# A four-layer trunk with routed experts: the test for crowded groups moved behind the last scatter

## The reference, cut to what matters

```python
scores = jax.nn.sigmoid((t @ router_w).astype(jnp.float32))
sel = scores + router_b.astype(jnp.float32)
group_score = lax.top_k(sel.reshape(-1, N_GROUPS, EXPERTS_PER_GROUP), GROUP_SCORE_TOPK)[0].sum(-1)
best_group = jnp.argmax(group_score, axis=-1)          # one of 4 groups for each token
_, e_idx = lax.top_k(jnp.where(in_group, sel, -jnp.inf), TOP_K)   # two of its 4 experts
...
hid = jax.nn.silu(jnp.einsum("td,edf->tef", t, w_gate)) * jnp.einsum("td,edf->tef", t, w_up)
out = jnp.einsum("tef,efd->td", hid * combine[..., None], w_down)
...
xs = _layer_norm(ALPHA * xs + (1 + m_s[5])[:, None] * fs, ln_ffn_g[l], ln_ffn_b[l])
```

## Time and profile before

| | |
|---|---|
| median of three runs | 2169.0 us (2166.23 to 2172.78) |
| span of the profiled execution | 2165.3 us |
| TensorE busy (matmul / weight load) | 2015.4 / 1403.3 us |
| VectorE busy | 1336.2 us |
| ScalarE busy | 1028.3 us |
| GpSimd busy | 246.3 us |
| mean granted TensorE clock | 0.975 |
| chain that ended last | PE 75%, DVE 16%, ACT 4%, issue 3%, DMA 1% |

### The profile page before, as it was taken

How to read it: one execution, slowest core, us unless ns; L and a number is a source line. 1 busy time by engine, 2 the same in 40 slices (tenths; PEclk the granted TensorE clock), 3 DMA queues, 4 the chain that set the end, 5 groups by cost and what they waited for, 6 DMA issues and landing times.

```text
span 2165.3 us, 45010 instructions
## 1 busy us (share of the span) xinstructions
PE 2015.4 (93%) x18880; PEld 1403.3 (65%) x18881; DVE 1336.2 (62%) x2625; ACT 1028.3 (47%) x1779; POOL 246.3 (11%) x363
## 2 busy tenths in 40 slices
PE   6999999899998999899899998998999999989996
PEld 4666666557776676587656665776566666647774
DVE  3666666437896342689832325898666666538896
ACT  3344334226774251576523314766444444326774
POOL 1422222110001000100010001000322232100000
PEclk8999999999999999999999999999999999999998
DMA  9244334345896444488734353888311121125880
GB/s 396 88 164 147 123 139 166 143 139 207 281 326 220 146 158 190 156 306 299 261 124 154 119 214 136 303 302 308 104 64 62 49 70 46 46 81 192 281 305 31
DMA packets 56911, 381.21 MB, mean 176 GB/s; under 512 B 6400, under 2 KB 10624, under 8 KB 12144
## 3 DMA queue, kind: packets, MB, share of 16 engines
q1 hardware_dynamic: 51696, 373.00, 48.2%
q10 hardware_dynamic: 4608, 4.20, 0.6%
q0 software_dynamic: 384, 0.89, 0.1%
HBM read 373.96 MB, written 4.10 MB: 175 GB/s over the span
## 4 chain that ended last, share of the span: by engine, by line
PE 75%; DVE 16%; ACT 4%; issue 3%; DMA 1%; SPq 0%; DVEq 0%; ACTq 0%
PE ps L846 15%; DVE e_wlo L2843 7%; PE ps L1513 5%; PE ps L1517 4%; PE ps L1516 4%; PE ps L796 4%; PE ps L772 4%; PE ps L752 3%; PE ps L987 3%; DVE bufx L2862 3%; PE ps L1300 3%; PE ps L1469 2%; PE ps L807 2%; ACT e_whi L1708 2%; PE ps L1401 2%
## 5 line engine op out<-in xcount | busy, mean ns | idle before, releaser
L2843 DVE TENSOR_TENSOR e_wlo<-ring,e_whi 128x1024 fp32r<-128x1024 f32 x384 | 455.1, 1220 | 71.7 <-ACT e_whi L1708 70.2
L1708 ACT ACTIVATE e_whi<-ring 128x1024 fp32r<-128x1024 f32 x384 | 402.5, 1060 | 114.6 <-PE ps L1517 111.5
L846 PE MATMUL ps<-bufh,ring 128*128 128x384 f32 x1024 | 390.6, 503 | 2.2 <-ACT scratch L1708 0.7
L1513 PE MATMUL ps<-e_whi,e_hs 128*128 128x512 f32 x512 | 211.0, 412 | 35.5 <-DVE e_wlo L2843 32.4
L846 PEld LDWEIGHTS ps<-bufh,ring 128*128 128x128 f32 x1024 | 176.3, 190 | 93.5 <-issue 17.5
L1708 ACT ACTIVATE scratch<-ps 128x384 f32<-128x384 f32 (+6 forms) x311 | 109.1, 368 | 212.9 <-PE ps L846 53.0
L1517 PE MATMUL ps<-e_whi,e_hs 128*128 128x512 f32 x512 | 200.7, 392 | 0.0
L1516 PE MATMUL ps<-e_wlo,e_hs 128*128 128x512 f32 x512 | 200.0, 391 | 0.0
L2980 POOL TENSOR_SCALAR bufx<-bufo,x_gb 128x384 f32<-128x384 f32 x56 | 37.6, 686 | 1061.9 <-DVE bufo L2279 1061.9
L1513 PEld LDWEIGHTS ps<-e_whi,e_hs 128*128 128x128 f32 x512 | 96.0, 188 | 77.4 <-ACT e_whi L1708 51.9
L2372 DVE SCALAR_TENSOR_TENSOR scratch<-scratch,par 128x386 f32<-128x386 f32 x192 | 128.4, 669 | 4.8
(11 more groups left out here) (311 smaller groups left out, 3488.8 us busy)
## 6 DMA issues: line engine op xcount, KB each, us to landing
ring<-in_moe SPq DMA_DIRECT2D x192, 1024.0 KB, 4.9
ring<-in_w_ada SPq DMA_DIRECT2D x96, 1024.0 KB, 6.3
ring<-in_gdn_w_in SPq DMA_DIRECT2D x32, 1024.0 KB, 7.0
ring<-in_gdn_w_out SPq DMA_DIRECT2D x8, 1024.0 KB, 5.0
ring<-in_gqa_w_in SPq DMA_DIRECT2D x6, 1024.0 KB, 5.0
ring<-in_gqa_w_out SPq DMA_DIRECT2D x4, 1024.0 KB, 7.3
ring<-in_mla_w_out SPq DMA_DIRECT2D x4, 1024.0 KB, 8.1
ring<-in_mla_w_in SPq DMA_DIRECT2D x3, 1024.0 KB, 5.0
```

The costliest lines, as they stand in the source:

```text
L846: last = mm(ps[:, head_bank(n, m), 0:T], w[:, m % 2, kt, :], bufh[:, kt, :], start=(kt == 0), stop=(kt == KT - 1))
L1513: first = mm(out, parts[0], whi, start=start, stop=False)
L1708: return op(out, in_, ACT.Copy, **kw)
L2843: return tt_(e_wlo[:, b, :], w, e_whi[:, b, :].bitcast(F32), ALU.subtract)
```

## The change

On TensorE and VectorE the call of `crowded_blocks` moves from ahead of the last group's scatter to behind the whole list of steps, which ends with the last scatter (TensorE) and the last additions (VectorE). Inside the crowded part, TensorE now waits until the last group's additions are done too. ScalarE's program, the flags, the semaphore counts and all loads stay.

```diff
@@ -1563,7 +1563,7 @@
                 with pe.If(crowded > 0):
                     pe.wait_ge(F["yhi"], 2 * NG * (l + 1))
                     pe.wait_ge(F["ylo"], 2 * NG * (l + 1))
-                    pe.wait_ge(F["sc_ev"], KT * (NG * (l + 1) - 1))
+                    pe.wait_ge(F["sc_ev"], KT * NG * (l + 1))
                     with pe.Fori(0, NG) as g:
                         for b in range(2):
                             n = g * 2 + (2 * NG * l + b)
@@ -1676,11 +1676,10 @@
                     else:
                         n = NG * l + j
                         if e == 0:
-                            if j == NG - 1:
-                                crowded_blocks(l, comb)
                             pe.wait_ge(F["ga_ev"], 16 * l + 16)
                         scatter_piece(F, n, e, e_put[:, j % 2, :], (6, 0, 1, 2) if j == NG - 1 else (5, 6),
                                       n * KT if n else None)
+                crowded_blocks(l, comb)
 
             for S in (F, X):
                 pe.sem_inc(S["wfree"], SPLITS)
@@ -2931,13 +2930,12 @@
                     elif kind == "y":
                         y_low(F, NG * l + j)
                     elif kind == "s":
-                        if e == 0 and j == NG - 1:
-                            crowded_blocks(l)
                         if e == 0 and l + j:
                             dve.wait_ge(F["sc_ev"], KT * (NG * l + j))
                         scattered(F, l, NG * l + j, e, (6, 0, 1, 2) if j == NG - 1 else (5, 6))
                         if e == 3 and j < 2:
                             put_back(j + 2)
+                crowded_blocks(l)
 
             dve.wait_ge(params_in, 16)
```

## The result

The changed kernel takes 2177.93 us in the median of 17 runs, the kernel before 2168.83 in 17 runs; the ratio is 1.0035, with a 95% interval of 1.0023 to 1.0048, so 5 to 10 us more, some 7.6 (the two medians lie 9.1 apart). The forecast was 2177.3 and "slower".

The account below looks back on a forecast made before the run. It took the serial chain after each layer's last down products as the bound. Later column sums and fold cost 21.9 us, earlier additions win 13.6: +8.3, so 2177.3 as a median, range 2166 to 2185.

Parts of the forecast that it names:

- The gain: Last additions into bufx: start 1.49 us after the low part without the test ahead, winning 13.6 us over four layers.
- The place of the read: TensorE's flag read behind the last scatter tile: starts 2.85 us after the first addition.
- The length of the test: TensorE's flag read and branch before the column sums: 4.9 us in every layer, bounds 3.7 and 6.5.
- The sums: TensorE's eight column sums after the test: one piece at half clock, 3.3 us, from 2 x 1.74 less a tail.
- The fold: TensorE's fold after the column sums: about 1.55 us at half clock instead of 0.91, 0.64 more a layer.
- the kinder rival: TensorE's test and sums: clock or branch kinder than forecast, about 2170 us; chance 0.22.
- The sum: Whole kernel: 21.9 us lost less 13.6 won, +8.3 us.
- VectorE's test: Behind VectorE's last additions: free, covered by 3.1 us of TensorE's delay; without that cover up to 2.4 us a layer.
- second stop: Behind the branch's jump: none counted in the sum, though VectorE's row in layer 2 suggested one of about 2.9 us.
- The faster rival: TensorE's branch: jump target already in its buffer, branch under about 2.2 us, time about 2160 us; chance 0.08.

Follow-up runs that it names:

- the other execution of the kernel before: The kernel before, unchanged, executed once more for its trace; its four changed places took 50.53 us in all.
- the busy TensorE: Changed kernel plus four matrix products into an unread bank, queued on TensorE just ahead of the flag read; 2175.20 us, ratio to before 1.0022.
- eight banks: Changed kernel with eight PSUM banks instead of four for the last scatter; 2156.35 us, ratio to before 0.9948.
- the changed kernel's two executions: The changed kernel's profiled execution, spanning 2176.1 us, and one with 128 no-ops added at the head of TensorE's program, 2179.69 us in one run.
- the first experiment: Kernel before with only VectorE's test moved behind its last additions, TensorE's left ahead of the scatter; 2169.89 us, ratio to before 1.0004.

## Why the prediction was right, point by point

**The gain.** Right. The additions came 1.64 after the start of the low part in all four layers; forecast 1.49. The gain was 13.0 (5.40 + 5.79 + 4.77 + 3.58 - 4 x 1.64) instead of 13.6. TensorE's first weight load stands 0.91 after the start of the low part, not 0.74; the rest, 0.73, was as estimated.

**The place of the read.** Right: 2.76 after the first addition (676.0 - 673.24), forecast 2.85.

**The length of the test.** From the read to the first column sum 6.1, 4.6, 5.0 and 4.7 us, 5.1 in the mean, forecast 4.9. Right in the mean, but the reason holds only in part: I took layer 3's length for all because no weights would be loading. Hardly any were (8 and 0 GB/s by layer 0's stretches above), and layer 0's branch was 4.57 all the same. Where loads had run beside the branch before, it did get shorter by 0.4 to 0.5 (5.01 to 4.57, 3.75 to 3.37, 4.31 to 3.80), and in layer 3, which had none, it didn't (3.40 and 3.45). But in the other execution of the kernel before layer 3 took 3.92, so whether the loads or the place made the difference, no run separates.

**The sums.** Mis-sized: 2.79 for 3.3. The piece takes 1.50 at full clock (the busy TensorE, eight banks), so the 1.74 of the earlier trace rows that I doubled was too long; VectorE was still making the last of its input beside it (L2258, until 470.13).

**The fold.** Right in layer 0 (1.65; forecast 1.55), wrong in the three others, where the clock had come back by then (0.91). In the other execution three of four were slow. So this term is worth 0.7 to 2.2 and not 2.6. Here the kinder rival, a clock that comes back sooner, had a part of the truth.

**The sum.** Forecast +8.3, measured +6.0 and +7.4 on the stage and +7.6 by the ratio of the runs. The error is in the sums (2 us too many) and the fold (0.4 to 1.9), partly offset by the smaller gain (0.6) and the longer test (20.5 in four layers for 19.6). So the mechanism was right, but that 2177.3 stands 0.6 beside the median of 2177.93 is luck: the sum was 1 to 2 us too high, and single runs of the changed kernel range from 2167.70 to 2186.97. The interval of the ratio also reaches below the 0.3% (2175.5) from which the prediction counts a time as slower.

**VectorE's test.** Right that it cost nothing here, and that its cover was TensorE's own delay: the experiment that took this delay away shows it at 0.7 to 1.2 a layer, for up to 2.4 in the prediction. One step was mis-sized: VectorE's sequencer read the flag 3.4 to 3.5 after the first addition (676.7 - 673.24 in layer 0), 1.8 before the additions end, and not at 4.8, half a microsecond before.

**The rivals.** The Trainium skill (Runtime: NRT & Kernel Launch, section Instruction fetch mechanics) calls the crossing of a page boundary "mostly hidden", from which I took it that no second stop follows the jump. TensorE had none in eight of eight places of the changed kernel's two executions; the kernel with 32 increments more had one of 1.3 us. VectorE's stop in layer 2, which I read as a second one of 2.9, was the only one of its test: the first increment ran at once (1514.8), the next came at 1517.3, so 2.5 us behind it. The faster rival needed a short branch; none came without emptying the part that is jumped over.

## What to carry to other kernels

What a branch on run-time data costs can depend on what it skips: here, on TensorE, 0.2 to 0.35 us over four instructions and 3.3 to 5.5 over a long block, whether in the old place or in the new one. Moving it is only worth something if the engine's work for the whole stall has been issued first; look at what keeps the queue from running ahead (here four banks, each waiting for an addition) and free that before moving. An engine whose test looks hidden may be covered by another engine's stall, so both must be costed again once the first is gone.

## What the runs showed of the hardware that I had not expected

- TensorE's compare-and-branch over the long part is itself recorded at 3.3 to 5.5 us, while VectorE's lasts 0.06 and the stop follows behind it (the branch at 1083.1, the first increment at 1085.8 in the first experiment).
- The first flag read of the program takes 0.48 to 0.55 us on each of the three engines, the later ones 0.27 to 0.32, in every kernel here that reads the flag.
- VectorE's stop can also fall among the increments. In layer 3 of the changed kernel the third increment ran at 2149.8 and the fourth at 2152.3:

```profile
L2903 DVEq EVENT_SEMAPHORE  x1: 21/21/21, 2149.8 to 2149.8; - x1
...
L2904 DVEq EVENT_SEMAPHORE  x1: 21/21/21, 2152.3 to 2152.3; - x1
```

  In layer 3 it stood behind the third increment in all seven traces with VectorE's test moved and the long part kept; with the test in its old place it stood behind the first increment of layer 2 in all four traces. So where it falls goes with the place in the program; what happens there, no row shows.
- TensorE stood 3.7 us after the dense scatter of the eight banks and kept its full clock; after the sparse scatter of the changed kernel and 5.6 us it ran at half. A dense scatter doesn't always save it: with the flag read earlier, TensorE stood 3.6 us behind the same scatter, began the sums at full clock and fell to half during them.
- A stop of 1.3 us followed some dozens of instructions behind the jump, in one execution of one kernel (32 increments more).
